# Decay sums of the gated recurrences: two levels at once, as rounded products in a high and a low part

## The reference, cut to what matters

```
S_t = exp(log_f_t) * S_(t-1) + k_t v_t^T          (decay per key dimension)
o_t = q_t S_t
```

## Time and profile before

| what | us |
|---|---|
| median of the runs | 1638.86 |
| lowest, highest run | 1636.62, 1638.98 |
| span of the profiled execution | 1639.4 |
| mixer of the first layer, from the place where D and A begin to alternate to its end | 77 to 235 |
| mixer of the second layer, same stretch | 500 to 659 |
| PE busy in these stretches | 152.0 of 158, 154.2 of 159 |

### The profile page before, as it was taken

One profiled execution on the slowest core, in us unless ns is written; L12 is line 12 of the kernel. 1 busy time (PEld: TensorE's weight loads), 2 busy tenths in 40 slices (PEclk: granted clock), 3 DMA queues, 4 the chain that ended last, 5 costly groups with the idle time before them and its releaser, 6 DMA issues.

```text
span 1639.4 us, 26865 instructions
## 1 busy us (share of the span) xinstructions
PE 1556.2 (95%) x10684; PEld 1326.6 (81%) x10684; DVE 1121.1 (68%) x1651; ACT 810.4 (49%) x1303; POOL 0.2 (0%) x4
## 2 busy tenths in 40 slices
PE   7999988999999989799999899899999989899998
PEld 7987567888898857688889788788888888688886
DVE  3865667886476666678855887877454798777535
ACT  3533255665535333655644455755345446655434
POOL 0000000000000000000000000000000000000000
PEclk9999999999999979899999899999999989999999
DMA  7421034665542201365654333455555333355552
GB/s 255 154 84 53 1 103 132 194 210 188 181 147 67 77 27 53 126 196 182 218 185 130 101 103 121 143 191 194 203 182 152 114 104 103 124 185 193 202 182 103
DMA packets 182203, 232.05 MB, mean 142 GB/s; under 512 B 22560, under 2 KB 153408, under 8 KB 181952
## 3 DMA queue, kind: packets, MB, share of 16 engines
q1 hardware_dynamic: 182080, 230.34, 43.4%
HBM read 229.28 MB, written 1.05 MB: 140 GB/s over the span
## 4 chain that ended last, share of the span: by engine, by line
PE 81%; DVE 9%; ACT 3%; DVEq 3%; DMA 2%; issue 2%; ACTq 1%; SPq 0%
PE banks L440 79%; DVE all_ring_rounded L2804 2%; DMA all_ring<-in_ffn_w_gate 1%; DVE all_ring_rounded L1645 1%; DVE all_rest L2973 1%; DVE all_work L2908 1%; ACT all_ring_rounded L1392 1%; DMA all_ring<-in_w_ple_gate 1%; DVEq L2907 1%; PE banks L954 1%; PE banks L2289 0%; DVE all_work L2892 0%; DVE all_work L2870 0%; DMA all_ring<-in_w_in 0%; ACT all_work L351 0%
## 5 line engine op out<-in xcount | busy, mean ns | idle before, releaser
L440 PE MATMUL banks<-all_work_rounded,all_ring_rounded 128*128 128x512 f32 (+2 forms) x4160 | 650.8, 318 | 15.1 <-DVEq L436 10.3
L440 PEld LDWEIGHTS banks<-all_work_rounded,all_ring_rounded 128*128 128x128 f32 (+1 forms) x4160 | 585.0, 190 | 78.9 <-DVEq L436 12.0
L440 PE MATMUL banks<-all_ring_rounded,all_work_rounded 128*128 128x512 f32 (+2 forms) x2304 | 501.2, 378 | 13.6 <-DVE all_ring_rounded L2804 10.2
L440 PEld LDWEIGHTS banks<-all_ring_rounded,all_work_rounded 128*128 128x128 f32 x2304 | 411.0, 193 | 94.8 <-DVE all_ring_rounded L2804 15.6
L2804 DVE TENSOR_TENSOR all_ring_rounded<-all_ring,all_ring_rounded 128x2048 fp32r<-128x2048 f32 x104 | 237.9, 2292 | 119.5 <-ACT all_ring_rounded L2622 117.2
L1645 DVE TENSOR_TENSOR all_ring_rounded<-all_ring,all_ring_rounded 128x2048 fp32r<-128x2048 f32 (+2 forms) x96 | 213.8, 2233 | 74.3 <-ACT all_ring_rounded L1392 72.7
L2622 ACT ACTIVATE all_ring_rounded<-all_ring 128x2048 fp32r<-128x2048 f32 x104 | 198.6, 1911 | 118.6 <-DMA all_ring<-in_w_mlp_down 86.9
L1392 ACT ACTIVATE all_ring_rounded<-all_ring 128x2048 fp32r<-128x2048 f32 (+2 forms) x96 | 177.9, 1860 | 111.1 <-DMA all_ring<-in_w_in 45.1
L440 PE MATMUL banks<-all_work 64*64 64x64 f32 (+8 forms) x2180 | 155.6, 272 | 20.2 <-ACT all_work L2626 9.0
L440 PEld LDWEIGHTS banks<-all_work 64*64 64x64 f32 (+5 forms) x2180 | 114.3, 152 | 62.4 <-issue 29.8
L440 PE MATMUL banks<-all_work,all_ring 128*128 128x128 f32 x704 | 102.8, 291 | 2.4 <-DVEq L409 1.9
(11 more groups left out here) (263 smaller groups left out, 1203.8 us busy)
## 6 DMA issues: line engine op xcount, KB each, us to landing
all_ring<-in_w_in SPq DMA_DIRECT2D x48, 1024.0 KB, 5.3
all_ring<-in_w_mlp_up SPq DMA_DIRECT2D x32, 1024.0 KB, 5.4
all_ring<-in_w_mlp_down SPq DMA_DIRECT2D x32, 1024.0 KB, 4.9
all_ring<-in_ffn_w_gate SPq DMA_DIRECT2D x22, 1024.0 KB, 5.5
all_ring<-in_ffn_w_up SPq DMA_DIRECT2D x22, 1024.0 KB, 5.6
all_ring<-in_ffn_w_down SPq DMA_DIRECT2D x22, 1024.0 KB, 4.9
all_ring<-in_w_out SPq DMA_DIRECT2D x16, 512.0 KB, 4.2
all_ring<-in_w_out SPq DMA_DIRECT2D x8, 1024.0 KB, 6.3
```

The source lines that it names most:

```text
L440: ins = self.nc.tensor.matmul(out, lhsT, rhs, start=start, stop=stop)
```

## The change

Three things change in `gla` of the first block, and a constant is rounded once.

1. The span matrices are rounded to fp32r in place, once, by one DVE copy at the start of the first layer. `log_f` (tokens on partitions) is split: ACT copies the bank rounded (`lf_tok`), DVE subtracts that from the bank (`lf_low`, rounded) in its third step. PE's level step 0 waits for `lf_low`; DVE's third step now waits for ACT's copy.
2. At even s, PE makes the spans of levels s and s+1 together: for each of `R` row tiles one bank, in which each half of the tokens gets two rounded products of 256 columns, one with the high and one with the low part. For A the first row tile is made at the start of the step, the second at its end. Both use the same bank, so the second waits for ACT's exponential of the first. ACT takes the exponentials of both levels at even s, one instruction of 512 columns per row tile, and does nothing at odd s. DVE waits for both row tiles. `e` holds four levels.
3. The zero products that open and close `o` are rounded ones.

```diff
-    g.e, g.K, g.Q = turn(2, 2, T), turn(2, 2, P), turn(2, 2, P)
+    g.e, g.K, g.Q = turn(4, 2, T), turn(2, 2, P), turn(2, 2, P)
...
+            def span(pair, r):
+                name = f"{g.name}_span{pair}{r}"
+                b = psum.claim(pe, name, for_span)
+                for t in range(NT):
+                    levels = spans[:, 6:9:2, :] if pair == 3 and t else spans[:, 2 * pair:2 * pair + 2, :]
+                    out, columns = b[:, 2 * t * P:2 * (t + 1) * P], slice(r * P, (r + 1) * P)
+                    mm(out, rounded(g.lf_tok)[:, t, columns], levels, True, False)
+                    last = mm(out, rounded(g.lf_low)[:, t, columns], levels, False, True)
+                last.then_inc(psum.full_of(name), 1)
             for s in range(LEVEL_STEPS):
                 if s == 0:
-                    pe.wait_ge(*due("lf_tok", m + 1))
+                    pe.wait_ge(*due("lf_low", m + 1))
+                    pe.wait_ge(spans_rounded, 1)
                     o = psum.claim(pe, g.name + "_o", for_o)
-                    mm(o[:, :], shaped(C("spans"), 9, P)[0:1, 0, :], shaped(C("spans"), 9, P)[0:1, 0:4, :], True, False)
-                if s < n:
-                    name = f"{g.name}_span{s}"
-                    b = psum.claim(pe, name, for_span)
-                    for r in range(g.R):
-                        for t in range(NT):
-                            last = mm(b[:, r * T + t * P:r * T + (t + 1) * P], g.lf_tok[:, t, r * P:(r + 1) * P],
-                                      spans[:, s + (t if s == n - 1 else 0), :])
-                    last.then_inc(psum.full_of(name), 1)
+                    mm(o[:, :], spans[0:1, 0, :], spans[0:1, 0:4, :], True, False)
+                if s < n and not s % 2:
+                    span(s // 2, 0)
...
+                if s < n and not s % 2 and g.R == 2:
+                    span(s // 2, 1)
                 yield
...
-            drain_bank(g.name + "_lf", g.lf_tok[:, :, :], "lf_tok", part=slice(0, NT * g.R * P))
+            act.wait_ge(*psum.filled(g.name + "_lf"))
+            A_(rounded(g.lf_tok), shaped(psum.bank(g.name + "_lf")[:, 0:NT * g.R * P], NT, g.R * P), ACT.Copy).then_inc(S["lf_tok"], 1)
...
-                if s < n:
-                    if s >= 2:
-                        act.wait_ge(*due("kq", n * m + s - 1))
...
+                if s < n and not s % 2:
+                    if s >= 4:
+                        act.wait_ge(*due("kq", n * m + s - 2))
+                    for r in range(g.R):
+                        name = f"{g.name}_span{s // 2}{r}"
+                        act.wait_ge(*psum.filled(name))
+                        A_(g.e[:, s % 4:s % 4 + 2, r, :].rearrange("p l (t c) -> p l t c", c=P),
+                           shaped(psum.bank(name), NT, 2, P).rearrange("p t l c -> p l t c"), ACT.Exp).then_inc(*psum.freed(name))
+                        act.drain().then_inc(S["e_ready"], 1)
...
             V.tensor_tensor(g.qk, g.q, g.k, ALU.mult)
+            dve.wait_ge(*due("lf_tok", m + 1))
+            V.tensor_tensor(rounded(g.lf_low), shaped(psum.bank(g.name + "_lf")[:, 0:NT * R * P], NT, R * P),
+                            as_float32(rounded(g.lf_tok)), ALU.subtract).then_inc(*psum.freed(g.name + "_lf"))
+            dve.drain().then_inc(S["lf_low"], 1)
...
-                    dve.wait_ge(*due("e_ready", n * m + s + 1))
+                    dve.wait_ge(*due("e_ready", n * m + R * (s // 2 + 1)))
...
         if not layer:
             dve.wait_ge(const_in, 16)
+            V.tensor_copy(rounded(C("spans")), C("spans")).then_inc(spans_rounded, 1)
```

More of the change, by code:

```diff
@@ L655 @@
     1, "b_exp": 1, "erow": 1, "hid": 1, "decays": 1, "nt": 1, "act": 2, "lb_max": 1, "lb_exp": 1, "ff_conv": 22, "ff_gate": 22, "ff_gelu": 22,
-    "kr_done": 1, "dve": 47, "log_f": 2, "lf_tok": 2, "e_ready": 16, "kq": 16, "masked": 14, "last_scores": 2, "weighed": 16, "level_U": 6,
+    "kr_done": 1, "dve": 47, "log_f": 2, "lf_tok": 2, "e_ready": 12, "lf_low": 2, "kq": 16, "masked": 14, "last_scores": 2, "weighed": 16, "level_U": 6,
     "ff_scaled": 22, "ff_prod": 22, "g_hi": 22, "ff_up": 22, "ff_added": 22,
@@ L791, in block1 @@
         ctx.enter_context(nc.semaphore(f"b1_{n}_in")) for n in ("constants", "columns", "mla_weights", "gain_rows"))
+    spans_rounded = ctx.enter_context(nc.semaphore("b1_spans_rounded"))
     def psum_of(layer):
@@ L869, in block1 @@
     g = bb_
-    g.Q, g.e, g.K = turn(2, 2, P), turn(2, 1, T), turn(2, 1, P)
+    g.Q, g.e, g.K = turn(2, 2, P), turn(4, 1, T), turn(2, 1, P)
     whole = shaped(turn.tensor[:, 0:3 * 2 * T], 3, 2, T)
@@ L874, in block1 @@
     g.q_apart, g.P, g.VF = turn(2, T), turn(2, 4, P), turn(2, GW)
-    g.lf_tok = shaped(g.lf.rearrange("p a b -> p (a b)"), NT, P)
+    g.lf_tok, g.lf_low = shaped(g.lf.rearrange("p a b -> p (a b)"), NT, P), turn(NT, P)
     g.spare, g.vtok = mixT[:, 4:5, :], hT[:, 4:6, :]
@@ L1047, in gla @@
             for_scores.sort()
-            spans, chosen, n = shaped(C("spans"), 9, P), shaped(C("chosen"), 5, CHUNK), len(LEVELS)
+            spans, chosen, n = shaped(rounded(C("spans")), 9, P), shaped(C("chosen"), 5, CHUNK), len(LEVELS)
+            def span(pair, r):
[7 more added lines that the diff above has]
+                last.then_inc(psum.full_of(name), 1)
             for s in range(LEVEL_STEPS):
                 if s == 0:
-                    pe.wait_ge(*due("lf_tok", m + 1))
+                    pe.wait_ge(*due("lf_low", m + 1))
+                    pe.wait_ge(spans_rounded, 1)
                     o = psum.claim(pe, g.name + "_o", for_o)
-                    mm(o[:, :], shaped(C("spans"), 9, P)[0:1, 0, :], shaped(C("spans"), 9, P)[0:1, 0:4, :], True, False)
-                if s < n:
-                    name = f"{g.name}_span{s}"
-                    b = psum.claim(pe, name, for_span)
-                    for r in range(g.R):
-                        for t in range(NT):
-                            last = mm(b[:, r * T + t * P:r * T + (t + 1) * P], g.lf_tok[:, t, r * P:(r + 1) * P],
-                                      spans[:, s + (t if s == n - 1 else 0), :])
-                    last.then_inc(psum.full_of(name), 1)
+                    mm(o[:, :], spans[0:1, 0, :], spans[0:1, 0:4, :], True, False)
+                if s < n and not s % 2:
+                    span(s // 2, 0)
                 if 2 <= s < n + 2:
@@ L1093, in gla @@
                     if l == n - 1:
-                        nothing = mm(o[:, :], shaped(C("spans"), 9, P)[0:1, 0, :], shaped(C("spans"), 9, P)[0:1, 0:4, :], False, True)
+                        nothing = mm(o[:, :], spans[0:1, 0, :], spans[0:1, 0:4, :], False, True)
                         nothing.then_inc(psum.full_of(g.name + "_o"), 1)
@@ L1710, in gla @@
                     c = LEVELS[s]
-                    dve.wait_ge(*due("e_ready", n * m + s + 1))
-                    V.tensor_tensor(packed(g.K[:, s % 2], c), firsts(g.e[:, s % 2], c), firsts(g.k, c), ALU.mult)
-                    last = V.tensor_tensor(packed(g.Q[:, s % 2], c), seconds(g.q_apart, c), seconds(g.e[:, s % 2], c).broadcast_to([P, 2, P // c, c]), ALU.mult)
+                    dve.wait_ge(*due("e_ready", n * m + R * (s // 2 + 1)))
+                    V.tensor_tensor(packed(g.K[:, s % 2], c), firsts(g.e[:, s % 4], c), firsts(g.k, c), ALU.mult)
+                    last = V.tensor_tensor(packed(g.Q[:, s % 2], c), seconds(g.q_apart, c), seconds(g.e[:, s % 4], c).broadcast_to([P, 2, P // c, c]), ALU.mult)
                     last.then_inc(S["kq"], 1)
```

2 lines of the change are left out of this document (1 added, 1 removed).

## The result

The changed kernel takes **1650.72 us** (median of six runs, 1647.80 to 1652.61); the kernel before, on the same chip, 1637.01 (1633.91 to 1638.98). The ratio is 1.0084, with a 95% interval of 1.0068 to 1.0099: 13.7 us slower. The forecast was 1640.6, in a range of 1631 to 1647. A later set of runs of the same kernel gave 1647.91 against 1636.64 (1.0058 to 1.0089), 11.3 us slower. The profiled execution took 1652.61 us; its span is 1650.8, 11.4 more than the span before. What lies around the span is not too small to be seen: each timed run of the changed kernel is 1.8 us longer than its own span, each of the kernel before 2.1 us. So the profiled execution of the kernel before, with a span of 1639.4, stands for some 1641.5 us, 4.5 above its median, and that of the changed kernel 1.9 above its own; this is why the spans differ by less than the medians.

A forecast was written before the change was run, and what follows sets the result against it. PE, four fifths of the chain, was taken as the bound wherever it isn't waiting. Layers +0.2 and -0.15 us made zero; 1639.4 + 0.05 + 1.7 for the clock gave 1641.1, less 0.5: 1640.6 us, range 1631 to 1647.

The forecast's parts named there:

- I take one loss in two: +1.7.: PE behind A4's new idle stretches, one per layer: one of the two brings half clock, costing 1.7 us.
- The rival that named this mechanism: PE behind new idling in A4 and B4: clock falls in both layers, 1.7 us each behind A4; 1645 us, 30%.
- A without the clock: Recurrence A, all steps s = 0 to 7 summed without clock effects: +0.6 us a layer.
- s = 0: A's first step: PE waits for DVE's subtraction, second row tile waits for ACT's first exponential; +2.7 us.
- s = 2 and 3: Recurrence A: the dropped span had covered a wait at s = 3, so only about 0.45 us is saved.
- s = 6: Recurrence A: ACT copies X only after the second exponential, so PE idles 1.45 us before D12.
- the closing zero: End of recurrence A, 147.5 us: the rounded zero product saves nothing, DVE's row being on the chain.
- At s = 4 two half pairs cost what one span did: 0.: Recurrence A on PE: the row tiles made at s = 4 cost as much as the old span, no change.
- The 0.121 us a product: PE's pace per rounded 256-column product; four make a two-level row tile, 0.49 us.
- B: -0.4 and -0.75 forecast: Recurrence B: step 0's wait +1.05 and +1.65 us by layer; later spans and closing zero save -1.45, second layer -0.95 more.
- I take 0: Clock around B4, already low: new idling could shift it either way by up to 2 us a layer; taken as 0.
- Rival 1: The saving gets through: A4's wait of 2.7 us and some 0.5 at s = 3 come back per layer; 1632.5 us, 24%.

The follow-up runs named there:

- e10_half_fill: The changed kernel with four unread rounded products filling PE's wait in recurrence A's step s = 0; 1641.61 us.
- e1_bank: The changed kernel with the second row tile of A's step s = 0 put into an empty score bank; 1637.63 us.
- e2: The changed kernel with nine unread rounded products of 512 columns filling PE's wait in A's step s = 0; 1642.85 us.
- e7: The changed kernel with second row tile (s = 0) in a score bank, ACT's X copy before s = 6 exponentials, DVE's third B step before D21; 1628.71 us.
- e4: The changed kernel with ACT copying D's X of the second round before the exponentials of A's step s = 6; 1644.16 us.
- e5: The changed kernel with DVE's third step of B ahead of its step D21 instead of behind it; 1645.70 us.

## Why the prediction was wrong

**The step that failed is the price and the number of the clock's falls.** "I take one loss in two: +1.7." That the clock may fall behind such a wait was seen; what a fall costs, and how often it comes, was wrong. The 1.7 came from one stretch of 3.4 us at another place, although the prediction itself named low stretches of some 10 and 16.3 us around B4, in the same trace. Here the low stretches behind A4 were 10.2 us (four) and 6.8 us (three); a fall of 10.2 made stretch A 4.3 us longer (115.8 against 111.5), one of 6.8 some 3.0 to 3.4. The changed kernel's four traced layers had 4.3, 4.3, 3.0 and 4.2 where I had 0.85 a layer. And one in two was too few: by the clocks of the ten runs the fall came nearly every time. The rival that named this mechanism (30%) had its place right and the same price of 1.7, so it ended at 1645, below the result.

The Trainium skill (TensorE: Matmul & The Clock Gate, section HAM oscillation) has gaps between groups of matmuls throw TensorE back, at a loss of half the cold time. The gaps that it describes are waits for DMA of about 3 to 5 us, longer than any wait here, so it does not say that a wait of 2.1 us is paid for; the traces show that it can be. They agree roughly on the loss: 4.3 for 10.2 us is 0.42, and PE idled in the first 0.6 us of the low stretch. Why it is not the full half of the rest is not shown.

**A without the clock: +0.6 forecast, +1.85 measured** (111.55 against 109.7). Set beside the kernel before, row by row (e10_half_fill, first layer, which has no fall), the steps cost, with the forecast in brackets: s = 0 +2.4 (2.7), s = 1 -0.9 (-0.9), s = 2 and 3 -0.4 (-0.45), s = 4 +0.9 (0), s = 5 -0.9 (-1.1), s = 6 +1.8 (1.45), s = 7 -1.1 (-1.1), the closing zero 0 (0). So the step of A that failed is "At s = 4 two half pairs cost what one span did: 0." Before, the span stood right ahead of the choice of values, and covered what the choice needs, DVE's masking of the scores in the bank:

```profile
111.21 1.16 PE L440 MATMUL banks<-all_rest,all_work 128*128 128x128 f32 x8
112.30 0.65 PE L440 MATMUL banks<-all_work,all_rest 128*64 128x256 f32 x4
```

In the changed kernel the shorter row tile leaves a wait for that masking (L1723), and the second row tile comes on top:

```profile
117.25 0.74 PE L440 MATMUL banks<-all_rest_rounded,all_work_rounded 128*128 128x256 f32 x4
118.61 0.65 PE L440 MATMUL banks<-all_work,all_rest 128*64 128x256 f32 x4 [0.62 <-DVE all_work L1723]
```

The prediction saw this wait at s = 3 and not at s = 4. The rest are small products that were too cheap. A row tile of two levels takes 0.53 us only where two stand together (86.93 to 87.99 for eight products in e1_bank); between other products it was 0.57 to 0.67 from start to start, not 0.49. The rounded zero product took 0.43 us, not 0.24. The 0.121 us a product came from 72 in a row, and was carried over to groups of four, although the same rows showed plain spans at 0.92 in one place and 1.09 in another. The waits that were forecast came: 2.14 us idle in A4 (2.8), 1.48 before D12 (1.45), and the DVE subtraction took 0.69 as said.

**B: -0.4 and -0.75 forecast, +1.2 and -0.8 measured, the clock included.** The wait was as said, 2.86 us, ended by DVE's subtraction. At like low clock (10.2 us) stretch B of the first layer is 71.3 both with the change (e2, e10) and without, so the waits ate all that the spans gave. For the clock there the prediction said "I take 0"; over twelve values on either side stretch B is 0.8 us a layer longer, of which the clock is a part that these few values do not set apart.

**The sum.** A 2 x 1.85 = 3.7, falls behind A4 2 x 4.0 = 8.0, B 2 x 0.8 = 1.6: 13.3 us, against 13.7 and 11.3 in the two sets of runs. The forecast had 1.2, -1.15 for B, and 1.7, together 1.75. The base was off by little: its three runs had a median of 1638.86, the six 1637.01.

**Rival 1 was right in its direction and not in its number.** Its condition was not given. Made by hand, in e1_bank, it gave 1637.6 where the rival had 1632.5. What e7 has beyond that, 1628.7, comes with the waits before D12 and B4, which the rival did not name.

## What to carry to other kernels

Put an idle stretch of the bounding engine down with two prices, its own length and what the clock does behind it; the second was the larger here (4.3 against 2.1 us), came nearly every time in the changed kernel, and a few filler products removed it. Take its price from the low stretches that the trace already has, the long ones too. Where a span of work shrinks, look for the wait that it covered (0.6 us at s = 4). When a producer is split into two halves that share one buffer, follow the consumer's list: the second half waits for all that stands ahead of the first half's reader. And before a good idea is dropped for a bad time, mend the waits that it brings: three edits of one line each turned 13.7 us slower into 8.2 us faster.

## What the runs showed that I had not expected

The same wait of 2.14 us, in the same place behind the same products, was followed by 10.2 us at the low clock in one execution and by none in another (e4, and e5's two layers). So a single profile does not tell what a change costs in the clock; the mean granted clock over the runs does (0.967 after, 0.975 before). And stretch A repeats closely once it is sorted by that: 111.5 to 111.6 in all six layers that have the changed recurrence A, its bare or filled wait, no repair and no fall, 115.8 to 115.9 in the four with a fall of 10.2 us; with a fall of 6.8 us it was 114.6 and 115.0. This is why differences of 1.5 us in A can be read from single profiles, although the runs of one kernel scatter by 2 to 15 us.
